# PEER layers with 392 dense prompt tokens instead of 400, eight more tokens gathered

## The chip, the cores and the metric

The kernel runs on one core of a Trainium2 chip. Its time is the device time of one launch in microseconds. Three runs of the kernel before gave 3549.24, 3555.11 and 3555.85 us; the median is 3555.11.

## The reference

The program is one inference step of a decoder trunk of two layers for 512 prompt tokens and 8 sample tokens, with a width of 1024, all in float32. Layer 0 mixes tokens with a gated MLP, layer 1 with sparse attention. Behind each of them stands a PEER layer, and the change is about that one:

```
q = (x @ w_q).reshape(T, 8 heads, 2, 128)
s1, s2 = q[:, :, 0] @ sub_k1.T, q[:, :, 1] @ sub_k2.T       # 128 keys each
v1, i1 = top_k(s1, 16);  v2, i2 = top_k(s2, 16)
top_s, top_pos = top_k(v1[..., :, None] + v2[..., None, :], 16)   # of 256 pairs
eidx = i1 * 128 + i2 at top_pos                             # 16 of 16384 experts a head
gate = softmax(top_s)
act  = gelu(einsum('thkd,td->thk', expert_u[eidx], x))
y    = einsum('thk,thkd->td', gate * act, expert_v[eidx])
```

## The kernel before

**Two ways to the same sum.** The prompt tokens 112 to 511 (`ND` = 400 of them, from `D0` = 112 on) take the dense way. All 16,384 experts are computed for them: in phase `s`, 128 slabs of 128 rows of `expert_u` are multiplied with the normed activations, the results go through GELU and to DRAM (`act_d`). The gates of these tokens, mostly zeros, are made as a table of 128 x 128 a token by a product of two one-hot matrices (`gates`, line 817), and go to DRAM as well (`gate_d`). In phase `y` activations and gates are read back in 16 groups of 8 slabs (`abuf`, `gbuf`), multiplied on VectorE (`weigh`), split into a high and a low part and multiplied with 128 slabs of `expert_v`. The prompt tokens 0 to 111 and the 8 sample tokens take the gathered way. They stand in 8 groups: group 0 holds the 8 samples (8 heads x 8 tokens = 64 partitions), groups 1 to 7 hold 16 prompt tokens each (8 x 16 = 128 partitions). For each of a group's 16 experts GpSimd gathers one row of `expert_u` per partition (an indirect DMA into one of four buffers `rows`), and VectorE takes its product with the token's activations (`dot`, line 1966): 128 dots a layer. In phase `y` the same is done with rows of `expert_v` (`value`, lines 1982 and 1985), and a matmul with `sel_t` or `sel_p` sums over the heads (`group_y`).

**Precision.** Every slab product is three float32r products, high by high, high by low and low by high. A dense slab is `dense` (line 681): 8 chunks x 3 = 24 matmuls of 128 x 128 by 400 columns into one bank. Slabs with all 520 tokens use `slab` (line 666): 48 matmuls of 260 columns. The weights come in through SP's queue into four buffers `raw`; ScalarE makes the high part (`w_hi`, line 1190), GpSimd (line 2411) or, in phase `y`, VectorE (line 2092) the low part `w_lo` in place. A slab's load is issued when the slab four before it is done.

**Order in phase s.** Each engine has its own program, and the order is written out by hand in slabs of TensorE. VectorE routes four blocks of 128 tokens (`routing`: top 16 of the scores, of the pair sums, the choice of experts, the gates). `between()` is called at twelve points of a routing, the hooks; each may hold a dot. Block b is routed in a window of `ROUTE_SLABS[b]` slabs; then TensorE turns the routes (`turn_route`, line 870) and 16 steps follow, each one slab and one half, that is eight tokens' gates: VectorE writes their one-hots (`one_hots`, lines 2001 and 2004), TensorE multiplies them (line 817), ScalarE takes them to `gout`, SP stores two halves at a time. `STEP_DOTS` says how many dots stand ahead of the one-hots of a step. Block 0 has no such steps: of its tokens only 112 to 127 are dense, and their two halves open block 1's steps. The halves left over follow block 3 (`LAST_STEPS`). `FETCH_AT` says at which slab GpSimd, after the slab's low part, issues each gather; the gather for dot i + 4 is due when dot i is. The activations of a group are turned to rows on TensorE by `group_h` (line 839) after all dots of the group before; the first dot of a group waits for it. After the third dot of a group VectorE spreads the next group's activations (`group_rows`, line 1952). The experts of groups 1 to 7 are ready after block 0 is routed: SP stores `route` to DRAM (`route_d`) and reads it back with partitions of head and token (`routeP`).

**Start of phase y.** VectorE weighs group 0 and takes its low parts before the phase. In the loop over the 128 slabs n = 8 j + c it weighs part c + 1 of group j + 1 (at c = 0 also part 0, which waits for the group's loads), makes the low part of slab n + 2, adds up the gathered values, and adds slab n to `x` (line 2121), which frees its bank.

**Attention tiles.** `attention()` multiplies 17 tiles of 128 columns with `slab` into two banks by turns. 15 of them are rotated: VectorE writes the scaled tile to `traw`, TensorE multiplies it with `rot` (line 973) into the tile's own bank, after the following slab, and VectorE multiplies the result with the sine (`rb`, line 2156), which frees the bank. The slab after the following one writes the same bank.

## Time and profile before

| | us |
|---|---|
| median of three runs | 3555.11 |
| the profiled execution | 3555.51 |
| its span | 3553.7 |
| TensorE matmuls busy | 3407.9 |
| VectorE busy | 2562.3 |
| GpSimd busy | 1879.6 |
| ScalarE busy | 1341.9 |

The profile shows one execution. Matmuls are pipelined, so the busy time of TensorE counts overlaps once and the mean of one matmul is longer than its share of the time. Times of single instructions are given from the span's start. Phase s of layer 0 lies at about 441 to 1134 us, phase y at 1134 to 1718, the attention tiles at 1718 to 1872; layer 1's PEER phases begin at about 2268 and 2962. The page's DMA line and the windows give how busy the 16 DMA engines were and what they moved.

### The profile page before, as it was taken

The page shows a single profiled execution, that of the slowest core. Times are in us where ns is not written, and L with a number is a line of the kernel's source. Part 1 is how long each engine was busy: PE and PEld are TensorE (multiplying, and loading weights), DVE is VectorE, ACT ScalarE, POOL GpSimd, SP SyncE. Part 2 cuts the span into 40 slices and gives each one's busy share as a digit, 9 for nine tenths or more (in the row PEclk, how much of TensorE's full clock was granted, in tenths as well). Part 3 has the DMA queues.
Part 4 walks back from the last instruction along what each step waited for, and adds up shares of the span by engine and source line. Part 5 has one row for each costly group of instructions (what it writes and reads, how often), then busy time and mean ns, then how long its engine had stood idle before and what let it go on. Part 6 is the DMA issues. An engine that isn't in the chain of part 4 may idle for free.

```text
span 3553.7 us, 60286 instructions
## 1 busy us (share of the span) xinstructions
PE 3407.9 (96%) x21261; PEld 3279.6 (92%) x21261; DVE 2562.3 (72%) x5458; ACT 1341.9 (38%) x1928; POOL 1879.6 (53%) x1236
## 2 busy tenths in 40 slices
PE   7999999999999999999888789999999999999998
PEld 7999999999999999999884459999999999999998
DVE  3342388898885788887568753598898867878885
ACT  3323243545453333333222363344444443333332
POOL 3434366565656655554452234466665666555552
PEclk9999999999999999999999899999999999999999
DMA  3222267888899999997335532468989899999994
GB/s 131 83 67 89 89 200 239 291 288 284 296 302 297 296 333 338 327 340 247 95 99 180 157 103 89 126 202 284 299 264 314 286 312 283 326 337 334 330 332 143
DMA packets 396185, 837.93 MB, mean 236 GB/s; under 512 B 58280, under 2 KB 218792, under 8 KB 395224
## 3 DMA queue, kind: packets, MB, share of 16 engines
q1 hardware_dynamic: 269232, 454.25, 39.2%
q0 software_dynamic: 73824, 264.29, 21.5%
q10 hardware_dynamic: 52880, 116.19, 9.7%
q8 instruction: 142, 2.33, 0.3%
q14 instruction: 107, 0.88, 0.1%
HBM read 724.80 MB, written 108.60 MB: 235 GB/s over the span
## 4 chain that ended last, share of the span: by engine, by line
PE 82%; DVE 8%; DMA 4%; issue 2%; ACT 2%; POOL 1%; ACTq 0%; SPq 0%; DVEq 0%; POOLq 0%
PE acc L681 54%; PE acc L666 16%; PE misc L817 5%; DMA raw<-slabs_in 2%; DMA rows<-u_in,expertP 1%; DVE rows L1966 1%; PE misc L922 1%; POOL w_lo L2411 1%; PE misc L1140 1%; PE misc L746 1%; DVE passed L2250 1%; PE misc L1104 0%; ACT w_hi L1190 0%; PE acc L1024 0%; DVE hot_gate L2004 0%
## 5 line engine op out<-in xcount | busy, mean ns | idle before, releaser
L2411 POOL TENSOR_TENSOR w_lo<-raw,w_hi 128x1024 fp32r<-128x1024 f32 x365 | 891.6, 2446 | 917.4 <-ACT w_hi L1190 916.1
L681 PE MATMUL acc<-h_hi,w_hi 128*128 128x400 f32 x3072 | 1071.6, 349 | 10.6 <-POOL w_lo L2411 6.2
L681 PE MATMUL acc<-h_hi,w_lo 128*128 128x400 f32 x3072 | 1060.5, 345 | 0.0
L681 PE MATMUL acc<-h_lo,w_hi 128*128 128x400 f32 x3072 | 1059.2, 345 | 0.0
L1190 ACT ACTIVATE w_hi<-raw 128x1024 fp32r<-128x1024 f32 x617 | 652.9, 1059 | 1074.6 <-DMA raw<-slabs_in 994.7
L681 PEld LDWEIGHTS acc<-h_hi,w_hi 128*128 128x128 f32 x3072 | 579.7, 189 | 15.4 <-ACT gelu L1322 7.7
L681 PEld LDWEIGHTS acc<-h_lo,w_hi 128*128 128x128 f32 x3072 | 580.1, 189 | 0.0
L681 PEld LDWEIGHTS acc<-h_hi,w_lo 128*128 128x128 f32 x3072 | 578.6, 188 | 0.1
L2092 DVE TENSOR_TENSOR w_lo<-raw,w_hi 128x1024 fp32r<-128x1024 f32 x252 | 360.2, 1429 | 176.7 <-ACT w_hi L1190 176.2
L1966 DVE CUSTOM_DVE_ANT_0 rows<-acc,rows 128x1024 f32<-128x1024 f32 (+1 forms) x256 | 309.8, 1220 | 172.1 <-DMA rows<-u_in,expertP 130.8
L681 PE MATMUL acc<-y_hi,w_hi 128*128 128x400 f32 x1024 | 357.1, 349 | 11.8 <-DVE x L2121 11.7
L681 PE MATMUL acc<-y_hi,w_lo 128*128 128x400 f32 x1024 | 355.7, 347 | 0.0
L681 PE MATMUL acc<-y_lo,w_hi 128*128 128x400 f32 x1024 | 355.4, 347 | 0.0
L1322 ACT ACTIVATE gelu<-acc 128x400 f32<-128x400 f32 x256 | 129.2, 505 | 581.4 <-PE acc L681 578.1
L2445 POOL DMA_INDIRECT rows<-v_in,expertP x224 | 219.2, 979 | 198.5 <-DVE acc L1985 107.7
L2453 POOL TENSOR_TENSOR h_lo<-abuf,h_hi 128x400 fp32r<-128x400 f32 x128 | 190.6, 1489 | 143.7 <-ACT h_hi L1369 142.6
L2004 DVE TENSOR_SCALAR hot_gate<-misc,idxT,gateT 128x128 f32<-128x128 f32 x800 | 263.4, 401 | 0.0
L2445 POOL DMA_INDIRECT rows<-u_in,expertP x224 | 218.4, 975 | 56.3 <-issue 26.6
L2453 POOL TENSOR_TENSOR y_lo<-abuf,y_hi 128x400 fp32r<-128x400 f32 x112 | 176.7, 1578 | 114.8 <-ACT y_hi L1369 113.6
L666 PE MATMUL acc<-h_hi,w_hi 128*128 128x260 f32 x912 | 191.8, 292 | 39.9 <-DVE rb L2156 16.7
L1343 ACT ACTIVATE gout<-misc 128x512 f32<-128x512 f32 x200 | 197.4, 1076 | 77.9 <-PE misc L817 77.9
L817 PE MATMUL misc<-hot_gate,hot 128*128 128x128 f32 x1600 | 202.4, 281 | 13.9 <-DVE hot_gate L2004 13.9
(353 smaller groups left out, 5522.4 us busy)
## 6 DMA issues: line engine op xcount, KB each, us to landing
raw<-slabs_in SPq DMA_DIRECT2D x617, 512.0 KB, 4.6
act_d<-gelu SPq DMA_DIRECT2D x256, 200.0 KB, 5.1
gate_d<-gout SPq DMA_DIRECT2D x50, 1024.0 KB, 7.0
abuf<-act_d ACTq DMA_DIRECT2D x128, 400.0 KB, 6.7
gbuf<-gate_d ACTq DMA_DIRECT2D x90, 384.0 KB, 6.4
gbuf<-gate_d ACTq DMA_DIRECT2D x30, 448.0 KB, 6.2
unit<-ck_in SPq DMA_DIRECT2D x72, 128.0 KB, 2.8
vquad<-cv_in SPq DMA_DIRECT2D x64, 128.0 KB
```

Source lines behind the costliest of these rows:

```text
L666: last = pe.matmul(acc[:, par, half, 0:HT], w[:, c, :], m(c)[:, half * HT:(half + 1) * HT], start=start and c == 0 and w is w_hi[r] and m ...
L681: last = pe.matmul(acc[:, 0, par, 0:ND], w[:, c, :], m(c), start=c == 0 and w is w_hi[r] and m is m_hi, stop=c == KC - 1 and w is w_lo[r])
L817: last = pe.matmul(misc[:, q, j * P:(j + 1) * P], hot1[par][:, t, :], hot_gate[par][:, t, :], start=True, stop=True)
L1190: act.activation(w_hi[r][:], raw[r][:], ACT.Copy).then_inc(hi_done, 1)
L1322: act.activation(gelu[:, par, :], acc[:, 0, par, 0:ND], ACT.Gelu_apprx_tanh).then_inc(acc_free_act, 1)
L1343: act.activation(gout[cpar][:, :, t0:t0 + 4].rearrange("p i t -> p t i"), misc[:, q, :].rearrange("p (t i) -> p t i", t=4), ACT.Copy).then ...
L1966: dve.tensor_tensor_reduce(out=row, in0=acc[0:n, 1], in1=row, scale=1.0, scalar=0.0, op0=ALU.mult, op1=ALU.add, accum_out=dots[0:n, g, k:k ...
L2004: last = dve.tensor_scalar(hot_gate[par][:, t, :], count_row, idxT[:, 1, t0 + t:t0 + t + 1], gateT[:, t0 + t:t0 + t + 1], ALU.is_equal, AL ...
L2092: dve.tensor_tensor(w_lo[r][:], raw[r][:], w_hi[r][:].bitcast(F32), ALU.subtract).then_inc(lo_done, 1)
L2411: pool.tensor_tensor(w_lo[r][:], raw[r][:], w_hi[r][:].bitcast(F32), ALU.subtract).then_inc(lo_done, 1)
L2445: pool.indirect_dma_start(out=rows[n % RB][0:rows_of], out_offset=None, in_=a[f"v{l}" if half else f"u{l}"], in_offset=bass.IndirectOffset ...
L2453: pool.tensor_tensor(y_lo[par][:, c, 0:ND], abuf[par][:, c, :], y_hi[par][:, c, 0:ND].bitcast(F32), ALU.subtract).then_inc(y_lo_done, 1)
```

## The change

392 prompt tokens take the dense way instead of 400. The eight tokens 112 to 119 join the samples in group 0, whose 128 partitions are now all used: the gathers, dots, values and turns of group 0 run on 128 partitions, and `sel_t` picks samples and prompt tokens apart. The number of groups, dots and gathers stays. Since the experts of these eight tokens are known only after block 0 is routed and its routes have been stored and read back (eight more loads, into `routeS`), no dot is left in window 0. All dots start in block 1's window, with new tables of hooks, steps, fetches and turns. Window 1 has 19 slabs instead of 20, and the scores of block 1 come two slabs earlier; group 1 is turned in block 1's first step, group 3 after ten slabs of window 2. In block 2 four dots follow the first one-hots. There are 49 halves a layer instead of 50. The gate table in DRAM and `gbuf` are flat, 24 whole pairs of halves and one single half at the end, and `weigh` is two multiplications, one of 384 columns and one of 8. In phase y the parts of group 1 are weighed from slab 1 on by `WEIGH_FIRST`. In the attention tiles the product with `rot` goes to banks 2 and 3 of `misc`; the next slab that writes the tile's bank no longer waits for `rb` of that tile, and each `rot` waits for the `rb` of the tile before.

```diff
-ND = 400
+ND = 392
+NMATE = D0 % TG
-        ROUTE_SLABS = [20, 20, 14, 14]
+        ROUTE_SLABS = [20, 19, 14, 14]
-        SLAB0 = [0, 20, 56, 86]
+        SLAB0 = [0, 20, 55, 85]
+        WEIGH_FIRST = [[], [0, 1], [2], [3], [4], [5], [6, 7], []]
-        WINDOW_DOTS = [16, 12, 16, 12]
+        WINDOW_DOTS = [0, 16, 16, 12]
+        HOOK_DOTS = [[0] * 12,
+                     [0, 0, 0, 0, 2, 2, 2, 2, 2, 2, 2, 2],
+                     [1, 2, 2, 2, 1, 0, 0, 1, 1, 1, 1, 0],
+                     [0, 1, 1, 1, 1, 1, 1, 1, 1, 1, 1, 2]]
-                     [0, 2, 2, 0, 1, 1, 2, 1, 1, 2, 1, 1, 2, 1, 1, 2],
-                     [0, 1, 2, 1, 1, 2, 1, 1, 2, 1, 1, 2, 1, 0, 2, 2],
-                     [0, 1, 2, 1, 2, 1, 2, 2, 1, 2, 2, 0, 1, 2, 1, 2]]
-        TURN_AFTER = {(1, 2): 2, (1, 15): 3, (2, 0): 4, (2, 12): 5, (3, 0): 6, (3, 10): 7}
-        WINDOW_AT = [[8, 10, 10, 11, 12, 13, 14, 15, 16, 18, 19, 19, 20, 20, 20, 21],
-                     [30, 31, 32, 33, 35, 36, 37, 38, 39, 39, 39, 40],
-                     [56, 57, 58, 60, 61, 62, 63, 64, 65, 67, 68, 68, 68, 69, 69, 70],
-                     [86, 87, 88, 90, 91, 92, 93, 93, 94, 96, 98, 99]]
+                     [0, 1, 2, 1, 2, 1, 2, 1, 2, 2, 2, 0, 2, 2, 2, 2],
+                     [0, 0, 2, 2, 2, 2, 0, 2, 2, 2, 1, 2, 2, 1, 2, 2],
+                     [0, 2, 2, 0, 2, 2, 2, 1, 2, 2, 1, 2, 2, 0, 2, 2]]
+        TURN_AFTER = {(1, 0): 1, (1, 10): 2, (2, 5): 4, (2, 15): 5, (3, 2): 6, (3, 12): 7}
+        TURN_IN = {2: (10, 3)}
+        WINDOW_AT = [[],
+                     [26, 26, 28, 28, 29, 29, 30, 31, 32, 32, 33, 34, 35, 35, 37, 37],
+                     [55, 58, 58, 59, 60, 61, 62, 63, 66, 67, 68, 69, 70, 70, 70, 71],
+                     [87, 88, 89, 90, 91, 91, 92, 92, 94, 95, 96, 97]]
-        FETCH_AT = [5] * RB + at_slab[:-RB]
-        FETCH_AT = [n if i < TOPK else max(n, 28) if i < NDOT else max(n, NK - 1) for i, n in enumerate(FETCH_AT)]
+        FETCH_AT = [24] * RB + at_slab[:-RB]
+        FETCH_AT = [n if i < NDOT else max(n, NK - 1) for i, n in enumerate(FETCH_AT)]
...
                     sp.dma_start(routeP[h * TG:(h + 1) * TG].rearrange("t g k s -> t g (k s)"),
+                    sp.dma_start(routeS[SR + h * NMATE:SR + (h + 1) * NMATE, :, 0], route_d[l][NSG * TG:D0, h]).then_inc(
+                        routeP_loaded, 16)
...
                 group_h(0)
-                s_only(17)
+                s_only(15)
                 scores(1, 0)
                 s_only(2)
                 scores(1, 1)
                 s_only(3)
                 turn_route(0)
-                s_only(4)
-                group_h(1)
...
+                    if s:
+                        pe.wait_ge(acc_free_dve, D0 + s + 2)
                     for half in range(2):
-                        last = pe.matmul(acc[:, par, half, 0:HT], rot[:], traw[par][:, half * HT:(half + 1) * HT],
+                        last = pe.matmul(misc[:, 2 + half, 0:HT], rot[:], traw[par][:, half * HT:(half + 1) * HT],
...
-                    slab(base + s, s % 4, s % 2, hh, hl, free=(acc_free_dve, D0 + s + 1),
+                    slab(base + s, s % 4, s % 2, hh, hl, free=(acc_free_dve, D0 + max(s, 2)),
...
+                            dve.scalar_tensor_tensor(expertS[SR:P], routeS[SR:P, 0, 0], float(NK), routeS[SR:P, 1, 0],
+                                                     ALU.mult, ALU.add).then_inc(expertP_done, 1)
-                        elif done[0] < last_dot and (b != 1 or hook[0] > 4):
+                        for _ in range(HOOK_DOTS[b][hook[0] - 1]):
                             next_dot()
...
                         one_hots(H0 + h, h * HG, h % 2, H0 + h < 2)
+                        while done[0] < last_dot:
+                            next_dot()
...
-                    dve.tensor_tensor(abuf[par][:, c, :].rearrange("p (n t) -> p n t", t=TG),
-                                      abuf[par][:, c, :].rearrange("p (n t) -> p n t", t=TG),
-                                      gbuf[par][:, :, c, :], ALU.mult).then_inc(y_mult, 1)
+                    dve.tensor_tensor(main, main, gbuf[par][:, 0:GT].rearrange("p (n g t) -> p n g t", g=GRP, t=TG)[:, :, c],
+                                      ALU.mult)
+                    dve.tensor_tensor(rest, rest, gbuf[par][:, GT:].rearrange("p (g t) -> p g t", g=GRP)[:, c],
+                                      ALU.mult).then_inc(y_mult, 1)
...
                     if j + 1 < J:
-                        if c == 0:
-                            weigh(j + 1, 0)
-                        if c + 1 < GRP:
-                            weigh(j + 1, c + 1)
+                        if j == 0:
+                            for k in WEIGH_FIRST[c]:
+                                weigh(1, k)
```

## Rows read from the trace of the kernel before

**Rows 1.** The page's costliest groups: busy us, mean ns of one, idle before.
```profile
L681 PE MATMUL acc<-h_hi,w_hi 128*128 128x400 f32 x3072 | 1071.6, 349 | 10.6 <-POOL w_lo L2411 6.2
```

**Rows 2.** The chain of waits in order of time: start us, length us, what.
```profile
349.13 86.52 PE acc L666 x720
...
569.20 34.95 PE acc L681 x192
...
1143.35 7.30 PE acc L681 x24
```

**Rows 3.** Who waited for whom, whole run, TensorE: us, times, longest us.
```profile
PE acc L666 <- DVE rb L2156: 16.7, 15, 4.0
...
PE acc L681 <- DVE x L2121: 14.9, 7, 4.6
PE misc L817 <- DVE hot_gate L2004: 13.9, 6, 2.7
```

**Rows 4.** Timeline of TensorE, layer 0, gate blocks: start us, us, instruction, idle before.
```profile
621.44 0.49 PE L870 MATMUL misc<-ident,route 128*128 128x128 f32 x3
...
629.05 1.16 PE L817 MATMUL misc<-hot_gate,hot 128*128 128x128 f32 x8 [2.72 <-DVE hot_gate L2004]
...
791.69 0.55 PE L870 MATMUL misc<-ident,route 128*128 128x128 f32 x3 [0.30 <-DVE route L1915]
...
798.23 1.06 PE L839 MATMUL acc<-ident,hS 128*128 128x128 f32 x8 [1.62 <-DVE dots L1966]
...
801.82 3.57 PE L817 MATMUL misc<-hot_gate,hot 128*128 128x128 f32 x15 [2.53 <-DVE hot_gate L2004]
...
810.92 1.95 PE L817 MATMUL misc<-hot_gate,hot 128*128 128x128 f32 x16
...
817.07 1.95 PE L817 MATMUL misc<-hot_gate,hot 128*128 128x128 f32 x16
```

**Rows 5.** Windows: length, busy us of PE, PEld, DVE, ACT, POOL, clock, DMA, GB/s.
```profile
797.00:908.00 111.00, 107.24 (x691) 106.97 (x692) 97.21 (x250) 55.56 (x69) 62.86 (x40) 0.97 0.87 281
...
1240.00:1340.00 100.00, 100.00 (x557) 100.00 (x556) 81.08 (x93) 33.63 (x45) 58.36 (x47) 1.00 0.92 334
```

**Rows 6.** DMA issues, whole run: count, median us from issue to landing.
```profile
rows<-u_in,expertP POOLq DMA_INDIRECT x224, 6.5
```

**Rows 7.** Timeline of VectorE, layer 0, routing and gate steps.
```profile
577.59 1.23 DVE L1966 CUSTOM_DVE_ANT_0 rows<-acc,rows 128x1024 f32<-128x1024 f32 x1 [11.06 <-DMA rows<-u_in,expertP]
...
721.16 3.18 DVE L1834 MAX8 keyv<-sc 128x8 f32<-128x128 f32 x16
728.58 1.23 DVE L1966 CUSTOM_DVE_ANT_0 rows<-acc,rows 128x1024 f32<-128x1024 f32 x1 [4.23 <-issue]
...
767.01 1.23 DVE L1966 CUSTOM_DVE_ANT_0 rows<-acc,rows 128x1024 f32<-128x1024 f32 x1
...
791.56 1.22 DVE L1966 CUSTOM_DVE_ANT_0 rows<-acc,rows 128x1024 f32<-128x1024 f32 x1
...
1070.17 1.22 DVE L2001 TENSOR_TENSOR hot<-misc,idxT 128x1024 f32<-128x1024 f32 x1
...
1073.85 1.22 DVE L2001 TENSOR_TENSOR hot<-misc,idxT 128x1024 f32<-128x1024 f32 x1
```

**Rows 8.** Timeline of TensorE, attention: a slab after a rotated tile.
```profile
1839.04 0.48 PE L666 MATMUL acc<-h_hi,w_hi 128*128 128x260 f32 x2 [0.88 <-DVE rb L2156]
```

**Rows 9.** DMA by queue, 1190 to 1250 us: packets, MB, share of 16 engines.
```profile
q0 software_dynamic: 1953, 7.09, 36.4%
```

**Rows 10.** Timeline of VectorE at the start of phase y, layer 0.
```profile
1132.39 0.16 DVE L2100 TENSOR_TENSOR weights<-dots,routeS 64x16 f32<-64x16 f32 x1
...
1137.95 0.57 DVE L2077 TENSOR_TENSOR abuf<-abuf,gbuf 128x400 f32<-128x400 f32 x1 [5.22 <-DMA abuf<-act_d]
```

**Rows 11.** DMA, 1130 to 1190 us: queue, packets, MB, share; issues, us to landing.
```profile
q0 software_dynamic: 1187, 3.90, 26.1%
...
rows<-v_in,expertS POOLq DMA_INDIRECT x15, 8.7
```

More of the change, by code:

```diff
@@ L477, in build @@
             for r, n in enumerate(STEP_DOTS[b]):
[L478 removed]
+                if (b, r) in TURN_AFTER:
                     assert len(at_slab) + n == TURN_AFTER[b, r] * TOPK
@@ L832, in group_h @@
                 def group_h(g):
-                    n = P if g else SR
+                    n = P
                     pe.wait_ge(hS_done, l * NGR + g + 1)
@@ L906, in peer @@
                             quarter_scores(b + 1, SCORE_STEPS.index(r))
-                    if b + 1 < NDB:
+                    if b + 1 in TURN_IN:
+                        slabs, g = TURN_IN[b + 1]
+                        s_only(slabs)
+                        group_h(g)
+                        s_only(ROUTE_SLABS[b + 1] - slabs)
+                    elif b + 1 < NDB:
                         s_only(ROUTE_SLABS[b + 1])
@@ L1443, in group_out @@
                 def group_out(g):
-                    n = P if g else SR
+                    n = P
                     act.wait_ge(rows_used, l * OPS + NDOT + (g + 1) * TOPK)
@@ L1973, in value @@
                 g, k = divmod(i, TOPK)
-                n = P if g else SR
+                n = P
                 u = l * OPS + NDOT + i
@@ L1990, in group_add @@
                 dve.wait_ge(s_y_done, l * NGR + g + 1)
-                t0, w = ((g - 1) * TG, TG) if g else (TP, TS)
-                dve.tensor_tensor(x[:, :, t0:t0 + w], x[:, :, t0:t0 + w],
-                                  misc[:, 2, 0:KC * w].rearrange("p (c t) -> p c t", c=KC), ALU.add).then_inc(
-                    s_y_added, 1)
+                y = misc[:, 2, 0:KC * TG].rearrange("p (c t) -> p c t", c=KC)
+                if g:
+                    parts = [(0, (g - 1) * TG, TG)]
+                else:
+                    parts = [(0, TP, TS), (TS, NSG * TG, NMATE)]
+                for c0, t0, w in parts:
+                    last = dve.tensor_tensor(x[:, :, t0:t0 + w], x[:, :, t0:t0 + w], y[:, :, c0:c0 + w], ALU.add)
+                last.then_inc(s_y_added, 1)
             def one_hots(half, t0, par, first):
@@ L2060, in peer @@
                         one_hots(H0 + h, h * HG, h % 2, H0 + h < 2)
+                        while done[0] < last_dot:
+                            next_dot()
                 for h in range(3 * HALF_STEPS, HALVES):
@@ L2107, in peer @@
                     if j + 1 < J:
-                        if c == 0:
-                            weigh(j + 1, 0)
-                        if c + 1 < GRP:
-                            weigh(j + 1, c + 1)
+                        if j == 0:
+                            for k in WEIGH_FIRST[c]:
+                                weigh(1, k)
+                        else:
+                            if c == 0:
+                                weigh(j + 1, 0)
+                            if c + 1 < GRP:
+                                weigh(j + 1, c + 1)
                     if n < NK - 2:
```

104 lines of the change are left out of this document (57 added, 47 removed).

## The prediction

> **What bounds the kernel now.** I read the page first. TensorE is busy 3407.9 of 3553.7 us, and its costliest groups are the dense matmuls of line 681: three of 3072 and three of 1024, 12,288 matmuls of 400 columns, of which one group stands in [rows 1]. The reader should not take 349 ns as their price, because they overlap. The chain of waits has stretches with nothing else in them: 192 matmuls of 400 columns in 34.95 us, a pitch of 182.0 ns, and 720 of 260 columns in 86.52 us, 120.2 ns [rows 2]. Next come TensorE's own waits [rows 3]: 16.7 us for `rb` in the attention tiles, 14.9 us for the adds into `x` in the value phase, 13.9 us for one-hots. Its timeline shows where those for one-hots fall: at the starts of the gate blocks [rows 4]. Last I read the engines beside it. The DMA engines are busy 0.87 of a gate block and 0.92 of the value phase [rows 5], and a gathered row set lands 6.5 us after its issue [rows 6]. VectorE's order in a routing window is in [rows 7]. So the end is set by TensorE nearly everywhere, with VectorE and DMA close behind; time goes where TensorE has less to do, and comes back where it must wait.
>
> **Columns.** From 260 to 400 columns the pitch grows by 61.8 ns, 0.442 ns a column; 8 columns fewer save 3.53 ns, and 12,288 matmuls 43.4 us [rows 1, 2]. At a granted clock of 1.00, the 2.4 GHz level, one column a cycle would save 3.33 ns, 41.0 us. I take **-42.2**, between both; a slab of 24 matmuls falls from 4.37 to 4.28 us. The Trainium skill (TensorE: Matmul & The Clock Gate, Back-to-back issue gap) gives sustained pitches of 81 ns at 128 columns and 131 ns at 512, 0.13 ns a column: by that the cut would be worth 12.8 us. The two pitches of this trace contradict it.
>
> **One half fewer.** A gate step lasts 6.15 us (810.92 to 817.07) [rows 4]; less 4.37 for its slab, the matmuls of the one-hots cost 1.78 us. Each layer has 49 halves for 50: **-3.6**.
>
> **Attention tiles.** `rot` no longer writes the bank that the next slab needs; that slab may start while VectorE still reads the product. Each tile shows a wait like the 0.88 us of [rows 8]; 15 of them make 16.7 us [rows 3]. What is late next is VectorE: it started `rb` of that tile 0.9 us before the slab at 1839.04 could start, has the sum and a reciprocal behind it, and is free again before the slab ends, so it hides; ScalarE's and GpSimd's parts are shorter still. The new wait of `rot` is for a read that ended a slab earlier. **-17** (bounds 0 and -20).
>
> **Dots moved.** Group 0 becomes 128 rows and its 16 dots leave window 0. There VectorE gets rid of 16 dots and a wait for rows, so block 0 is routed early; scores of block 1 come two slabs sooner. SP issues eight more small loads, in two lots of eight, past which it moves a slab load and a store of activations each; a slab load is issued four slabs ahead and lands in about one, so I give this nothing (if the cover fails, 2 us a layer).
>
> Block 1. The first gathers are due at slab 24 instead of 28, but routing begins earlier too; where VectorE waited 11.06 us for them [rows 7] I expect some 8. Routing by itself is 791.56 - 721.16 - 4.23 = 66.2 us with 12 dots and one spreading of rows [rows 7], so 51.4 without; with 16 dots, one spreading and the wait it is 51.4 + 18.2 + 1.1 + 8 = 79, against 20 slabs, 86 us, until TensorE asks for it. Before, four dots stood behind the routing and TensorE waited 2.72 us for the first one-hots [rows 4]; now none do. With the clock that such a wait costs, **-6** for both layers (bounds 0, -9).
>
> Block 2. Dot 48 opens group 3 and must wait until TensorE has turned its rows, which now happens after ten slabs of the window: 10 x 4.28 + 0.9 = 43.7 us after the window's first slab. From the dot at 767.01 to the end of routing at 791.56 VectorE took 24.6 us with five dots [rows 7]; now it has four and one group's rows to spread, the same. Routing ends at 68.3. TensorE arrives after 14 slabs and the turn, 60.9: it waits 7.4 us. Behind the waiting dot on VectorE stands `topd`, behind that on ScalarE the exponential and two high parts; these are 3 us late and the slab that needs them is 8 us off. Four dots now stand between the first and second one-hots: 4 x 1.14 + 3.68 (the pitch 1070.17 to 1073.85) = 8.2 against 6.06 for TensorE's step, some 1 us more. The old cost was 0.30 + 1.62 + 2.53 of waits [rows 4] and about 3 us of half clock (the gate matmuls took 3.57 for 1.95 us). New: 7.4 + 0.6 + 1 + 3 = 12.0 against 7.4, **+9** for both layers (bounds 0, if the clock stays up and VectorE's later dots hide behind the slower TensorE, and +16).
>
> Block 3 and the steps. The window is 60.0 us and routing 66.2, less the lead with which VectorE begins: in block 2 it was 791.69 - 61.2 - 721.16 = 9.3 us [rows 4, 7], and 6.2 are enough. 24, 28 and 24 dots sit in the steps where 20, 20 and 23 did; a two-dot step costs VectorE 3.68 + 2.28 = 5.96 of TensorE's 6.06. Gathers issued in block 2's steps rise from 21 to 29. At 1.46 us of all DMA engines each (36.4% of 60 us for 15) [rows 9] the load of that block, 0.87 x 111 = 97 us, becomes 109 in 107 us [rows 5]. I take **+3** (bounds -4, +16), as a few late rows like those of before.
>
> **Value phase, start.** VectorE stood 5.22 us in `weigh` of group 1 for its loads [rows 10]; behind it were the low parts of slab 2, and TensorE waited 4.6 us [rows 3] and then took 7.30 us for a slab worth 4.37 [rows 2]. Moved behind slab 0, that wait is uncovered from TensorE. Late next is the slab load itself, since the DMA engines are full here. And group 0's 16 gathers grow: 15 of 64 rows cost 26.1% of 60 us, 15 of 128 rows 36.4% [rows 9, 11], so 6.2 us of DMA time more in each layer. **-5** for both (bounds -16, +12).
>
> **Value phase, rest.** 256 more multiplications of 8 columns at about 0.1 us [rows 10] lie on VectorE, which is busy 0.81 [rows 5]: nothing. The DMA share goes from 0.92 to 0.94 as the slab shortens: **+4** for late loads (bounds 0, +21).
>
> Sum: -42.2 - 3.6 - 17 - 6 + 9 + 3 - 5 + 4 = -57.8. The profiled execution took 3555.51 us, 1.8 more than its span and 0.4 above the median of 3555.11: **3498**.
>
> **Rivals.**
> *The DMA engines hold the value phase at its old pace.* 334 GB/s at a share of 0.92 [rows 5] leave room up to 363, and the shorter slab wants about 341; that speaks against. For it: shares of 0.94 to 1.0 at the phase's start, with gathers that land after 8.7 us [rows 11]. The columns of this phase, 21.1 us, and the 5 at its start are lost: 3524. The Trainium skill (DMA: Bandwidth & Descriptors, Specifications) puts the HBM limit of a core at 358 GB/s; it would let 341 pass too.
> *Slower: rows late in two-dot steps.* 64 steps of the two layers have two dots. With four row buffers a buffer comes round every 12.1 us, and issue, dot, descriptor work and a `w_lo` ahead of it in GpSimd's queue need 11.3 at 6.5 us of landing. From about 7.5 us the gate matmuls wait in each. At the 8.7 us of [rows 11] it is 1.4 us; in 45 of the 64 steps 63 us, and some clock: 3565. Against: in 100 gate steps TensorE waited six times for one-hots, 13.9 us in all [rows 3].
> *The cuts are given back at block starts.* TensorE's waits in all blocks are as block 2's (-6 becomes +9, +3 becomes +10): 3520.
> *Columns are cheap*: TensorE's pitch has a floor that hides them, 0.13 ns each, 29.4 us less gained: 3527. These would be the Trainium skill's pitches, cited above. Against: at 260 columns the same pair of weight load and matmul passes in 120.2 ns [rows 2], so no such floor lies above that.
>
> **Numbers.** Forecast 68 in 100, DMA 15, late rows 7, block starts 7, cheap columns 3. Late rows can reach 3600, the forecast's good bounds 3465; I give 3472 to 3528. About 0.2% (7 us) is what a measurement can tell: faster 0.89, within 0.04, slower 0.07.
>
> **What would show it.** Right: a pitch near 178.5 ns; no wait for `rb` in the tiles; no wait at the first gates of block 1; one of 5 to 9 us for `route` at block 2; slabs 2 and 3 of the value phase without the 4.6 us. Wrong: a DMA share of 1.0 and slab loads over 9 us in the value phase, waits of gate matmuls in many steps, or a pitch above 180 ns.

## The result and the profile after

The changed kernel takes 3534.51 us, the median of five runs (3517.39 to 3535.91), beside 3555.11 for the kernel before (3549.24 to 3558.76): a ratio of 0.9931, 95% interval 0.9907 to 0.9955. In a second lot of runs it stood at 3528.29 against 3551.67, ratio 0.9927 (0.9905 to 0.9949). The medians lie 21 and 23 us apart, and the two intervals together reach from 16 to 34 us. The forecast was 3498, 57 us less than before, with a range from 3472 to 3528: the direction held, the size did not, and the time lies outside the range. Executions of one and the same kernel differ here by 10 us and more to either side, the longer ones mostly at a lower mean clock (0.975 to 0.979) than the shorter (0.983 to 0.987); so below, stretches of the traces are compared, and the medians only where they are far apart.

From here on the starts of the 512 dense slabs on TensorE's timeline cut both traces into stretches. They are worked out from the first and the last matmul of each, in us, layer 0 / layer 1:

| stretch | before | after | difference |
|---|---|---|---|
| start of s to first step of block 1 (40 and 39 slabs) | 180.8 / 180.8 | 172.5 / 172.5 | -8.3 / -8.3 |
| 16 steps of block 1 | 108.3 / 108.3 | 104.4 / 104.3 | -3.9 / -4.0 |
| window 2, with the wait for `route` | 62.0 / 61.6 | 70.3 / 69.5 | +8.3 / +7.9 |
| 16 steps of block 2 | 111.2 / 111.2 | 115.4 / 114.6 | +4.2 / +3.4 |
| window 3 | 66.5 / 66.0 | 64.4 / 63.9 | -2.1 / -2.1 |
| 16 steps of block 3 | 103.7 / 102.3 | 101.7 / 104.6 | -2.0 / +2.3 |
| rest of s (11 and 12 slabs) | 56.2 / 56.7 | 57.7 / 58.2 | +1.5 / +1.5 |
| **phase s** | 688.7 / 686.8 | 686.5 / 687.6 | -2.2 / +0.8 |
| phase y, 8 slabs | 44.5 / 42.6 | 39.5 / 39.3 | -5.0 / -3.3 |
| phase y, 120 slabs | 543.7 / 545.5 | 537.1 / 539.1 | -6.6 / -6.4 |
| layer 0's last slab to layer 1's first | 550.1 | 551.0 | +0.9 |

With 0.4 us more ahead of the first slab and 1.2 behind the last they give the spans, 3553.7 and 3533.5. So in this pair of traces all that was won was won in phase y, -21.3; both phases s together made 1.4, and the attention stage lost 0.9. The forecast had -18.7 for the two phases s, -22.1 for the two phases y and -17 for attention.

Who TensorE waited for, whole run, to be held against [rows 3]: us, times, longest us.

```profile
PE misc L831 <- DVE hot_gate L2034: 22.3, 16, 3.9
PE misc L884 <- DVE route L1937: 17.1, 4, 8.6
...
PE acc L695 <- DVE x L2162: 13.7, 17, 3.6
...
PE misc L985 <- issue: 7.2, 2, 5.0
```

The line for `rb` (16.7 us) is gone. In its place stand three that were smaller or not there: one-hots 22.3 for 13.9, `route` 17.1, nearly all of it at block 2, where it had been 0.3, and 7.2 in which the sums of a tile wait for ScalarE. The group of the costliest matmuls, the row of [rows 1], and two rows of the chain, start and length, the answer to [rows 2]:

```profile
L695 PE MATMUL acc<-h_hi,w_hi 128*128 128x392 f32 x3072 | 1065.0, 347 | 10.2 <-POOL w_lo L2452 5.8
```
```profile
349.51 86.50 PE acc L680 x720
...
540.74 72.98 PE acc L695 x408
```

72.98 us for 408 matmuls are 178.9 ns each for 182.0 before, and 86.50 / 720 = 120.1 ns at 260 columns is what it was. The eight columns are worth 3.1 ns by these rows and 3.4 by the mean over all unbroken pairs on the timeline (182.2 and 178.7 ns). The two sustained pitches that the Trainium skill gives (TensorE: Matmul & The Clock Gate, Back-to-back issue gap: 81 ns at 128 columns, 131 ns at 512) would have made it 1.0; the traces disagree.

Windows: length, busy us of PE, PEld, DVE, ACT, POOL, clock, DMA share, GB/s. Window 2 with the turn of its routes, the steps of block 2, and the value phase, as [rows 5]:

```profile
716.00:788.00 72.00, 63.43 (x365) 63.06 (x363) 63.39 (x265) 26.08 (x34) 47.37 (x28) 0.95 0.82 267
788.00:902.00 114.00, 106.01 (x674) 104.73 (x675) 94.17 (x207) 54.07 (x68) 64.89 (x44) 0.95 0.85 285
...
1240.00:1340.00 100.00, 100.00 (x566) 99.76 (x566) 82.68 (x118) 35.88 (x48) 59.15 (x48) 1.00 0.95 345
```

The value phase moves 345 GB/s for 334 at a DMA share of 0.95 for 0.92, and TensorE is busy throughout this window; the DMA engines let the shorter slab pass here. The steps of block 2 are another matter: TensorE lacks 8 of 114 us and its clock is 0.95.

### Block 2 on three timelines

TensorE, layer 0, start us, us, instruction, idle before; the rows that answer to [rows 4]:

```profile
787.99 0.90 PE L884 MATMUL misc<-ident,route 128*128 128x128 f32 x3 [8.57 <-DVE route L1937]
794.32 1.95 PE L831 MATMUL misc<-hot_gate,hot 128*128 128x128 f32 x16
802.97 2.05 PE L831 MATMUL misc<-hot_gate,hot 128*128 128x128 f32 x16 [2.44 <-DVE hot_gate L2034]
813.21 3.14 PE L831 MATMUL misc<-hot_gate,hot 128*128 128x128 f32 x13 [3.90 <-DVE hot_gate L2034]
```

VectorE, the same time. Only dots (L1992) and the first part of the one-hots (L2031) are copied:

```profile
762.37 1.22 DVE L1992 CUSTOM_DVE_ANT_0 rows<-acc,rows 128x1024 f32<-128x1024 f32 x1 [5.04 <-issue]
...
789.65 1.23 DVE L2031 TENSOR_TENSOR hot<-misc,idxT 128x1024 f32<-128x1024 f32 x1 [1.72 <-ACT gateT L1422]
...
793.34 1.22 DVE L1992 CUSTOM_DVE_ANT_0 rows<-acc,rows 128x1024 f32<-128x1024 f32 x1
...
794.48 1.22 DVE L1992 CUSTOM_DVE_ANT_0 rows<-acc,rows 128x1024 f32<-128x1024 f32 x1
...
798.00 1.23 DVE L1992 CUSTOM_DVE_ANT_0 rows<-acc,rows 128x1024 f32<-128x1024 f32 x1 [1.14 <-DMA rows<-u_in,expertP]
...
799.14 1.22 DVE L2031 TENSOR_TENSOR hot<-misc,idxT 128x1024 f32<-128x1024 f32 x1
...
806.85 1.22 DVE L1992 CUSTOM_DVE_ANT_0 rows<-acc,rows 128x1024 f32<-128x1024 f32 x1 [3.94 <-DMA rows<-u_in,expertP]
```

And GpSimd, whose queue holds low parts (L2452) and gathers (L2485):

```profile
790.64 2.38 POOL L2452 TENSOR_TENSOR w_lo<-raw,w_hi 128x1024 fp32r<-128x1024 f32 x1 [10.45 <-ACT w_hi L1209]
793.17 0.95 POOL L2485 DMA_INDIRECT rows<-u_in,expertP  x1
798.36 2.39 POOL L2452 TENSOR_TENSOR w_lo<-raw,w_hi 128x1024 fp32r<-128x1024 f32 x1 [4.24 <-ACT w_hi L1209]
800.91 0.95 POOL L2485 DMA_INDIRECT rows<-u_in,expertP  x1 [0.15 <-issue]
```

Read from the top: VectorE stands 5.04 us before dot 48, because TensorE turns that group's rows after ten slabs of the window (the row names no releaser; with the turn after twelve slabs, below, the same row stands 13.97). The routes come late by that and TensorE stands 8.57 us. A slab buffer comes free only when a slab is done, so through this wait no slab is loaded, and GpSimd stands 10.45 and then 4.24 us on low parts. Behind the first one-hots VectorE has four dots. Three find their rows in the buffers, the fourth waits 1.14 us. The buffers of the first three are free from 794.5 us on, but the gathers that refill them stand in GpSimd's queue behind the low part of 798.36 and leave at 800.91. The next dot gets its rows at 806.85, 5.9 us later, which is no more than the 6.5 us of [rows 6]: the rows left late, they did not travel long. The second and third one-hots are late, TensorE stands 2.44 and 3.90 us more, and its gate matmuls then run at 3.14 us for the 13 that the row holds, where sixteen take 1.95, the granted clock being at its lower level, 1.2 GHz.

### The profile page after: what moved, and what is told of

Read it like the earlier page. It is cut to its first block, busy times and chain, and to the rows that moved or that the text cites. A ratio compares the mean times of both kernels' runs of the same rounds, so it can differ in the third digit from the quotient of the medians.

```text
span 3533.5 us, 60285 instructions
## 1 busy us (share of the span) xinstructions
PE 3371.9 (95%) x21229; PEld 3230.7 (91%) x21229; DVE 2597.1 (74%) x5702; ACT 1323.7 (37%) x1914; POOL 1845.2 (52%) x1236
## 3 DMA queue, kind: packets, MB, share of 16 engines
q1 hardware_dynamic: 269930, 452.21, 38.9%
q0 software_dynamic: 77920, 281.07, 22.3%
## 4 chain that ended last, share of the span: by engine, by line
PE 72%; DVE 13%; DMA 6%; issue 3%; ACT 2%; POOL 2%; SPq 1%; ACTq 0%; DVEq 0%; POOLq 0%
PE acc L695 47%; PE acc L680 15%; PE misc L831 3%; DMA rows<-u_in,expertP 3%; DMA raw<-slabs_in 2%; DVE rows L1992 1%; DVE hot_gate L2034 1%; POOL w_lo L2452 1%; ACT w_hi L1209 1%; PE misc L1159 1%; DVE route L1925 1%; DVE misc L1921 1%; PE misc L939 1%; PE misc L1123 1%; DVE w_lo L2129 1%
## 5 line engine op out<-in xcount | busy, mean ns | idle before, releaser
L2452 POOL TENSOR_TENSOR w_lo<-raw,w_hi 128x1024 fp32r<-128x1024 f32 x365 | 896.0, 2458 | 926.8 <-ACT w_hi L1209 925.4
L695 PE MATMUL acc<-h_hi,w_hi 128*128 128x392 f32 x3072 | 1065.0, 347 | 10.2 <-POOL w_lo L2452 5.8
L695 PE MATMUL acc<-h_lo,w_hi 128*128 128x392 f32 x3072 | 1048.0, 341 | 0.0
L695 PE MATMUL acc<-h_hi,w_lo 128*128 128x392 f32 x3072 | 1044.6, 340 | 0.0
L1992 DVE CUSTOM_DVE_ANT_0 rows<-acc,rows 128x1024 f32<-128x1024 f32 x256 | 308.6, 1219 | 158.8 <-DMA rows<-u_in,expertP 125.9
L695 PE MATMUL acc<-y_hi,w_hi 128*128 128x392 f32 x1024 | 353.4, 345 | 11.5 <-DVE x L2162 10.2
L695 PE MATMUL acc<-y_lo,w_hi 128*128 128x392 f32 x1024 | 350.0, 342 | 0.0
L695 PE MATMUL acc<-y_hi,w_lo 128*128 128x392 f32 x1024 | 348.9, 341 | 0.0
L2485 POOL DMA_INDIRECT rows<-v_in,expertP x224 | 213.4, 953 | 252.6 <-DVE acc L2011 119.0
L1341 ACT ACTIVATE gelu<-acc 128x392 f32<-128x392 f32 x256 | 127.4, 497 | 545.1 <-PE acc L695 536.5
L2493 POOL TENSOR_TENSOR h_lo<-abuf,h_hi 128x392 fp32r<-128x392 f32 x128 | 179.5, 1402 | 134.5 <-ACT h_hi L1391 133.1
L2485 POOL DMA_INDIRECT rows<-u_in,expertP x224 | 214.3, 957 | 66.3 <-issue 31.9
L831 PE MATMUL misc<-hot_gate,hot 128*128 128x128 f32 x1568 | 198.7, 281 | 22.6 <-DVE hot_gate L2034 22.3
L831 PEld LDWEIGHTS misc<-hot_gate,hot 128*128 128x128 f32 x1568 | 191.9, 196 | 29.5 <-DVE hot_gate L2034 29.4
```

The source lines that it names most:

```text
L695: last = pe.matmul(acc[:, 0, par, 0:ND], w[:, c, :], m(c), start=c == 0 and w is w_hi[r] and m is m_hi, stop=c == KC - 1 and w is w_lo[r])
L831: last = pe.matmul(misc[:, q, j * P:(j + 1) * P], hot1[par][:, t, :], hot_gate[par][:, t, :], start=True, stop=True)
L1341: act.activation(gelu[:, par, :], acc[:, 0, par, 0:ND], ACT.Gelu_apprx_tanh).then_inc(acc_free_act, 1)
L1992: dve.tensor_tensor_reduce(out=row, in0=acc[0:n, 1], in1=row, scale=1.0, scalar=0.0, op0=ALU.mult, op1=ALU.add, accum_out=dots[0:n, g, k:k ...
L2452: pool.tensor_tensor(w_lo[r][:], raw[r][:], w_hi[r][:].bitcast(F32), ALU.subtract).then_inc(lo_done, 1)
L2485: pool.indirect_dma_start(out=rows[n % RB][:], out_offset=None, in_=a[f"v{l}" if half else f"u{l}"], in_offset=bass.IndirectOffsetOnAxis(a ...
```

## The experiments

All are edits of the changed kernel unless the heading says otherwise. Ratios are to the kernel before. Those of the first four runs share one lot of runs of it (median 3551.67), the next four another (3552.42), the last two a third (3554.44).

### The changed kernel again

> The changed kernel once more, unchanged, to see where its own executions differ: three of its five took 3534.5 to 3535.9 us at a mean clock of 0.978, two 3517.4 and 3519.5 at 0.981 and 0.983. Theory: the 17 us are TensorE's clock after the attention tiles, where the profiled execution shows 0.55, 0.87, 0.97 in three stretches of 50 us and the kernel before 0.69, 1.00, 1.00; an execution near 3518 us would show the sample attention (from the last tile to the next layer's first slab) 8 to 12 us shorter than 405.2 us. Rival: the difference is spread over the gate layers, whose late rows differ from one execution to the next; then the sample attention stays at 405 in either.

Measured: 3528.29 us (3522.01 to 3533.78). The profiled execution has a span of 3526.6 and 541.3 us between the layers' slabs, 9.7 less than the first trace of the same kernel; its phases s took 684.8 and 688.8, its phases y 581.1 and 577.5, together +3.1. Two stretches of the sample attention, first trace and then second:

```profile
1961.00:2011.00 50.00, 33.91 (x177) 20.57 (x175) 30.25 (x100) 16.43 (x53) 9.66 (x11) 0.55 0.25 82
2011.00:2061.00 50.00, 46.60 (x400) 23.00 (x398) 31.82 (x144) 31.06 (x112) 30.86 (x33) 0.87 0.56 171
```
```profile
1965.00:2015.00 50.00, 32.72 (x228) 20.76 (x226) 33.40 (x120) 20.90 (x71) 12.19 (x13) 0.69 0.31 94
2015.00:2065.00 50.00, 46.16 (x442) 24.02 (x434) 34.92 (x148) 34.71 (x115) 33.86 (x37) 1.00 0.64 192
```

The granted clock is 0.55 in the one and 0.69 in the other, then 0.87 and 1.00. So nearly 10 us of the first trace's attention stage are a difference between executions of one program and no effect of the change. Block 2 differs as well: its window took 70.3 us again in layer 0 but 73.7 in layer 1, where TensorE waited 12.0 us for `route`; the largest difference on VectorE's timeline is one instruction of the routing (L1910) that took 2.49 us in place of 0.28, and why is open. The theory holds for the trace; that it explains every spread of 17 us is not shown, since the other executions left no trace.

### `rot` alone, on the kernel before

```diff
+                    if s:
+                        pe.wait_ge(acc_free_dve, D0 + s + 2)
-                        last = pe.matmul(acc[:, par, half, 0:HT], rot[:], ...
+                        last = pe.matmul(misc[:, 2 + half, 0:HT], rot[:], ...
-                    slab(... free=(acc_free_dve, D0 + s + 1),
+                    slab(... free=(acc_free_dve, D0 + max(s, 2)),
-  dve.tensor_tensor(halves(rb[:]), acc[:, par, :, 0:HT], ...
+  dve.tensor_tensor(halves(rb[:]), misc[:, 2:4, 0:HT], ...
```

> The kernel before with one part of the change alone: rot writes the third and fourth misc bank and the next slab no longer waits for rb. The prediction gave it -17 us (0 to -20). Theory A (from the changed kernel's trace, where the tiles took 8.9 us less and 5.0 of a wait for sqh stood where 4.0 for rb had been): -9 us in the tiles, and what comes after depends on the clock, so -9 in all or 0 to -3 if the sample attention then runs at a lower clock as in the changed kernel. Rival B: the prediction's -17, and the missing 8 us are from other parts of the change.

Measured: 3543.14 us over twelve runs, ratio 0.9972 (0.9953 to 0.9991), 10 us less, between 3 and 17. Its attention stage took 538.4 us for 550.1. Who TensorE waited for between the layers:

```profile
PE misc L968 <- issue: 6.1, 3, 4.6
```

The 16.7 us for `rb` are gone and 6.1 for the sums of a tile have come. The theory read from the trace, -9, is the nearer; -17 lies at the very edge of the interval. The tiles by themselves, from the start of the first slab to that of the seventeenth, took 144.2 us in the kernel before, 129.7 with this edit, and 130.5 to 132.6 in seven traces of the changed kernel and its edits below that leave this part alone.

### Index keys behind the square

```diff
-                    if 1 <= s < 1 + 4 * NU:
-                        load_index_keys(s - 1)
                     if TILES[s][0] in NORMED:
                         ...
                     if s:
                         after(s - 1)
+                    if 1 <= s < 1 + 4 * NU:
+                        load_index_keys(s - 1)
```

> The changed kernel with ScalarE's loads of index keys (four issues of some 0.9 us in each tile) behind its square and root of the same tile instead of before them. In the changed kernel's trace one tile's square waited 3.4 us behind such issues, and TensorE 5.0 us for it, at the only place in the tiles where it stood long; the clock fell after it. Theory A: that wait shrinks to 1.6 us or less, -4 us, and with the clock that comes back -5 to -15. Theory B: the late slab (raw landed 12.4 us after ScalarE was free) is the cause and the order hides nothing: 0. Rival C: index keys arrive later and the sample attention's start waits for them: +2 to +5.

Measured: 3518.36 us (3507.01 to 3537.26), ratio 0.9890 (0.9867 to 0.9913). ScalarE around the square that TensorE waits for, in the changed kernel (ACTq rows are issues):

```profile
1767.96 1.06 ACT L1209 ACTIVATE w_hi<-raw 128x1024 fp32r<-128x1024 f32 x1 [12.43 <-DMA raw<-slabs_in]
1768.64 3.77 ACTq L1552 DMA_DIRECT2D ik<-cki_in  x4
1772.46 0.60 ACT L1566 ACTIVATE sqh<-acc 128x520 f32<-128x520 f32 x1 [3.44 <-issue]
```

and TensorE at that tile, first in the changed kernel and then with the edit:

```profile
1773.16 2.07 PE L985 MATMUL misc<-sqh,headones 128*128 128x260 f32 x4 [5.01 <-issue]
```
```profile
1773.73 1.11 PE L985 MATMUL misc<-sqh,headones 128*128 128x260 f32 x4 [1.24 <-issue]
```

The wait falls from 5.01 to 1.24 us, 3.8 of it being the issues. The 1.24 that stay are the late slab, so for this wait theory A holds with theory B as its rest. The tiles took 123.9 us by the measure above, and 123.4 and 123.2 in the two kernels further down that have this edit too: 7 to 9 us less than in the seven others. But the clock did not come back. From the seventeenth slab through the sample attention to the next slab of this kind, these three traces took 268.0, 264.4 and 266.5 us, where eight of the nine without the edit took 255.5 to 260.1, and the ninth, the first of the changed kernel, 269.7. Here are 70 us in the middle of that stretch, with the edit and then with the turn after 8 slabs (columns as in [rows 5]):

```profile
1955.50:2025.50 70.00, 54.55 (x308) 29.81 (x306) 40.99 (x155) 26.82 (x96) 21.80 (x23) 0.60 0.35 109
```
```profile
1952.70:2022.70 70.00, 51.13 (x408) 30.19 (x406) 49.58 (x192) 34.87 (x123) 26.94 (x29) 0.83 0.43 134
```

TensorE's waits there add up to 44 to 48 us in all of them, so rival C, late index keys, is out, and the difference is the granted clock, 0.60 for 0.83. In these traces, then, the gain was given back. Whether the edit brings the low clock with it or three executions fell that way is not shown; each of the three was the slowest execution of its kernel. The interval of the whole time touches the changed kernel's; the 10 us between the medians are likely and not shown.

### Turn after 8 slabs, and after 12

```diff
-        TURN_IN = {2: (10, 3)}
+        TURN_IN = {2: (8, 3)}        # the other kernel: (12, 3)
```

> The changed kernel with the rows of group 3 turned after 8 slabs of block 2's window instead of 10. VectorE stood 5.0 us before dot 48 for them, so route should be ready 4.5 to 5 us earlier and TensorE's wait of 8.6 and 7.7 us fall to about 3.5. Theory A, a wait of TensorE feeds on itself: while it stands, no slab buffer comes free, GpSimd's queue stands on a low part and the gathers behind it are issued late, so VectorE stands for rows and TensorE again for one-hots (2.4 and 3.9 us, with 0.86 of clock); with the first wait halved these go too, -20 us for both layers. Theory B, each wait is its own: -10 us, and the one-hot waits of steps 2 and 3 of block 2 stay. Theory C, the four dots between first and second one-hots are the whole cost: 0 to -4 us, since the later waits then come at the same place.

> The changed kernel with the rows of group 3 turned after 12 slabs of block 2's window instead of 10: dot 48 and what is behind it on VectorE come 8.6 us later in each layer. If each wait is its own (as the turn after 8 slabs showed: wait for route 4.8 and 3.1 us shorter, the 16 steps behind it unchanged at 115.5 and 115.2), the window grows from 70.3 and 69.5 to 79 us, and the steps stay at 115: +17 us. If a long wait feeds itself through GpSimd's queue, the steps grow as well, to 120 and more: +25.

| turn after | median | ratio | window 2 | steps of block 2 |
|---|---|---|---|---|
| 8 slabs | 3515.27 | 0.9899 (0.9872 to 0.9925) | 65.6 / 67.9 | 115.5 / 115.2 |
| 10 slabs | 3528.29 | 0.9927 (0.9905 to 0.9949) | 70.3 / 69.5, again 70.3 / 73.7 | 115.4 / 114.6, again 114.3 / 115.2 |
| 12 slabs | 3542.86 | 0.9980 (0.9962 to 0.9998) | 78.9 / 78.9 | 114.6 / 114.5 |

TensorE's waits in window and steps of layer 0, turn after 8 slabs:

```profile
PE misc L831 <- DVE hot_gate L2034: 7.5, 3, 5.3
PE misc L884 <- DVE route L1937: 3.8, 1, 3.8
```

Turn after 12 slabs:

```profile
PE misc L884 <- DVE route L1937: 9.7, 1, 9.7
PE misc L831 <- DVE hot_gate L2034: 7.1, 3, 4.2
PE acc L695 <- POOL w_lo L2452: 5.5, 1, 5.5
```

Theory A, that the first wait makes the later ones larger with its own length, falls: the steps behind it take 115 us whether TensorE waited 3.8, 8.6 or 9.7. Theory B holds, the window alone follows the turn, by 5 us in layer 0 and, in layer 1, by 2 to 6: there 1.3 us went to a new wait of TensorE for the dots ahead of a turn. At 12 slabs part of it shows as another wait of 5.5 us, for a low part that GpSimd began at 775.14 us, 1.6 us after dot 48 had ended. That dot frees the buffer of the gather ahead of it in the queue; this is read from the order of the queue, no row names it.

### The gathers one slab earlier; the four dots moved away

```diff
-                     [55, 58, 58, 59, 60, 61, 62, 63, 66, 67, 68, 69, 70, 70, 70, 71],
+                     [55, 58, 58, 59, 60, 61, 62, 63, 66, 67, 68, 69, 69, 69, 69, 70],
```

> The changed kernel with the gathers of dots 56 to 59 put one slab earlier into GpSimd's queue, ahead of a low part instead of behind it. In the changed kernel's trace that low part waits until 798.4 us for its slab while the buffers of these rows are free from 794.5; the gathers leave at 800.9 and VectorE stands 3.9 us for the first. Theory A, late gathers: VectorE's wait of 3.9 us goes, TensorE's waits for one-hots in steps 2 to 4 of block 2 (2.4 and 3.9 us) fall below 3, the 16 steps of block 2 take 110 to 112 us instead of 115.4, -8 to -10 us for both layers with the clock. Theory B, the four dots between the first and second one-hots: TensorE's 2.4 us stay, the 3.9 shrink to about 2: -4. Theory C, the block's own gathers keep the DMA engines full (0.98 to 1.03 here), so rows land as late as before: 0.

```diff
-        WINDOW_DOTS = [0, 16, 16, 12]
+        WINDOW_DOTS = [0, 16, 12, 12]
-                     [0, 0, 2, 2, 2, 2, 0, 2, 2, 2, 1, 2, 2, 1, 2, 2],
+                     [0, 1, 2, 2, 2, 2, 1, 2, 2, 2, 2, 2, 2, 2, 2, 2],
-        TURN_AFTER = {..., (2, 5): 4, ...}
+        TURN_AFTER = {..., (2, 7): 4, ...}
-                     [55, 58, 58, 59, 60, 61, 62, 63, 66, 67, 68, 69, 70, 70, 70, 71],
+                     [55, 58, 58, 59, 60, 61, 62, 63, 66, 67, 68, 69],
```

> The changed kernel with no dots between the first and second one-hots of block 2: its four go to steps 0 to 15, 28 dots there for 24, group 4 turned after step 7 instead of 5. Theory A, late gathers: the second one-hots come 4.6 us sooner, but rows are then due in the same places, so the waits move to later steps, 0 to -4 us for both layers. Theory B, the four dots: TensorE's wait of 2.4 us goes and the 3.9 falls to nothing, -10 us. Rival: with two dots in nearly every step VectorE has 5.96 of 6.06 us in each, catches up nothing, and the waits spread: +5.

Earlier gathers: 3517.60 us, ratio 0.9894 (0.9869 to 0.9918); the steps of block 2 took 110.1 and 111.0. Moved dots: 3511.72, ratio 0.9896 (0.9869 to 0.9923), 110.7 and 110.4. Window 2 took 70.3 or 70.4 us in both layers of both. With the earlier gathers GpSimd and then VectorE read, where the changed kernel had 798.36, 800.91 and 806.85:

```profile
795.66 0.93 POOL L2485 DMA_INDIRECT rows<-u_in,expertP  x1 [0.72 <-DVE dots L1992]
...
800.14 2.38 POOL L2452 TENSOR_TENSOR w_lo<-raw,w_hi 128x1024 fp32r<-128x1024 f32 x1 [1.06 <-ACT w_hi L1209]
```
```profile
804.12 1.23 DVE L1992 CUSTOM_DVE_ANT_0 rows<-acc,rows 128x1024 f32<-128x1024 f32 x1 [0.97 <-DMA rows<-u_in,expertP]
```

TensorE's steps with the dots moved:

```profile
786.85 0.90 PE L884 MATMUL misc<-ident,route 128*128 128x128 f32 x3 [8.57 <-DVE route L1937]
793.12 1.95 PE L831 MATMUL misc<-hot_gate,hot 128*128 128x128 f32 x16
799.19 1.95 PE L831 MATMUL misc<-hot_gate,hot 128*128 128x128 f32 x16
805.26 1.95 PE L831 MATMUL misc<-hot_gate,hot 128*128 128x128 f32 x16
```

The gather leaves 5.3 us sooner (795.66 for 800.91), VectorE's wait falls from 3.94 to 0.97, and the 16 steps lose 4 to 5 us. With the dots moved the first steps pass at 6.07 us without a wait. Each expectation was half met: the gathers gave 8.9 us over both layers, as the theory of late gathers said, but TensorE's one-hot waits fell to 4.0 and not below 3; the moved dots gave as much, 8.9, where that theory allowed 4. The spread is small beside that: in all twelve stretches with neither edit (the changed kernel twice, both turns, the keys behind the square and the weighing of the next section) the 16 steps took 114.3 to 116.1 us. Read together, the two are one cause seen from its two ends. Four dots in a row empty the four row buffers while the queue that refills them stands, and either an earlier refill or a later demand cures it.

### Group 1 weighed from slab 0

```diff
-        WEIGH_FIRST = [[], [0, 1], [2], [3], [4], [5], [6, 7], []]
+        WEIGH_FIRST = [[0, 1], [2], [3], [4], [5], [6], [7], []]
```

> The changed kernel with group 1 weighed from slab 0 on, as in the kernel before. By the prediction's own step VectorE stands some 5 us for the loads of that group with the low parts behind it, and TensorE waits 4.6 us after slab 2: the first eight slabs of a value phase take 43 instead of 39.4 us, +3.5 us in each layer, +7. Rival: the slab loads themselves are late there, with DMA shares near 1.0, and the order changes nothing: 0 to +2.

Measured: 3530.55 us, ratio 0.9937 (0.9914 to 0.9960), which can't be told from the changed kernel's. In its trace the first eight slabs of phase y took 42.1 and 41.8 us, beside 39.5, 39.3, 40.5 and 38.9 in the two traces of the changed kernel: +2.4 in each layer. That is less sure than it looks. The other edits keep the new order too, and over all 18 stretches with it the eight slabs took 38.5 to 42.3 us, 40.1 on average; so the order is worth about 2 us in each layer, some 4 in all, and the spread of the stretches is as large. The expectation failed on the cause: with the old order VectorE does not stand for the loads of group 1 at all, it weighs at once and then stands for gathered rows of `expert_v`:

```profile
1128.27 0.56 DVE L2113 TENSOR_TENSOR abuf<-abuf,gbuf 128x384 f32<-128x384 f32 x1
...
1134.44 1.29 DVE L2008 TENSOR_SCALAR misc<-rows,weights 128x1024 f32<-128x1024 f32 x1 [3.21 <-DMA rows<-v_in,expertS]
```

And in the changed kernel:

```profile
1134.53 1.29 DVE L2008 TENSOR_SCALAR misc<-rows,weights 128x1024 f32<-128x1024 f32 x1 [1.10 <-DMA rows<-v_in,expertS]
1138.30 1.29 DVE L2011 SCALAR_TENSOR_TENSOR misc<-rows,weights,misc 128x1024 f32<-128x1024 f32 x1 [2.48 <-DMA rows<-v_in,expertS]
1139.49 0.56 DVE L2162 TENSOR_TENSOR x<-x,acc 128x392 f32<-128x392 f32 x1
```

TensorE waits 3.56 us for that add, where it waited 4.6 before and 5.0 with the old order. In either order it is the first gathered rows of `expert_v` that hold it, and no longer the loads of group 1. Which part of the change made those loads come in time is open.

### The edits together

One kernel has the turn after 8 slabs, the earlier gathers and the keys behind the square; in the other the moved dots take the place of the earlier gathers.

> The changed kernel with three edits together: group 3 turned after 8 slabs, the gathers of dots 56 to 59 one slab earlier, ScalarE's loads of index keys behind its square. Sum of the parts if each wait is its own: -10 for the turn (its trace showed the wait for route 3.8 and 4.6 us instead of 8.6 and 7.7), -8 for the gathers, -5 to -10 for the order in the tiles: 3528 - 25 = 3503. If one late row follows the other whatever is moved, 3515, where the two single edits stand already.

> Three edits on the changed kernel: group 3 turned after 8 slabs, the four dots behind the first one-hots of block 2 moved into its steps, ScalarE's loads of index keys behind its square. The version with the earlier gathers in place of the moved dots stood at 3500.4 us, its steps of block 2 at 114.4 and 109.2 us; moved dots took them to 110.7 and 110.4. If the moved dots are the steadier cure: 3496 to 3500. If both only shift the same late rows: 3500 to 3505.

Measured: 3500.40 us (3491.81 to 3511.12), ratio 0.9845 (0.9820 to 0.9870), and 3500.67 (3500.43 to 3508.79), ratio 0.9855 (0.9829 to 0.9882). Both beat the changed kernel by 28 us, clear of its interval, and the kernel before by 52 and 54. The medians nearly add up: -13, -11 and -10 by the single edits, -28 together. The traces of these executions, each the slowest of its five, account for less: beside the two traces of the changed kernel the two phases s together lost some 18 us in the first and 13 in the second, and the attention stage took 536.6 and 538.7 us, where three kernels without the keys' edit (the two turns and the old weighing) had 536.6 to 537.4. The window took 62.7 and 67.4 us in the first, 66.1 and 65.2 in the second; the steps of block 2 took 114.4 and 109.2, and 110.0 and 108.6. In layer 0 of the first a late row came back. Its gather left at 787.26 us, behind a low part that had waited until 784.73, and after the shorter wait the dots were there sooner than it could land:

```profile
792.83 1.23 DVE L1992 CUSTOM_DVE_ANT_0 rows<-acc,rows 128x1024 f32<-128x1024 f32 x1 [3.16 <-DMA rows<-u_in,expertP]
```

The moved dots look like the steadier cure, 108.6 to 110.7 us in all four stretches with them, though no difference of the medians says so.

## Why the prediction was wrong

**Columns, -42.2: right.** 182.2 to 178.7 ns over 12,288 matmuls is some 42 us, and 38 by the chain's rows. The rival of cheap columns is out.

**One half fewer, -3.6: right.** The rest of phase s has one slab more and one half fewer: +4.28 for the slab, -0.9 for the columns of eleven, leaves -1.8 of the measured +1.5 in each layer.

**Attention tiles, -17: mis-sized, -10 by the medians, -12 to -14 in the tiles of the traces.** The wait for `rb` went, as said. "What is late next is VectorE [...] ScalarE's and GpSimd's parts are shorter still" failed. ScalarE's own work is short, but its queue also issues four loads of index keys a tile, 3.5 to 3.8 us, ahead of the square. One tile's wait of 4.0 us had been put down to `rb` and came back as 5.0 under another name. The experiment on the kernel before gave -10 us. That the profiled pair shows +0.9 is the clock behind the tiles, 0.55 in the first trace against 0.69 in the second, whose stage took 541.3 us.

**Block 1, -6: right.** No wait for first one-hots (1.2 and 0.8 us for later ones); its steps lost 3.9 us, 1.4 of it columns, so -5 for both layers.

**Block 2, +9: the step that failed, +29.** Window 2 grew by 8.3 and 7.9 us, 9.5 and 9.1 with the columns it should have saved; the steps grew by 4.2 and 3.4, 5.6 and 4.8 with theirs. The wait for `route` was forecast at 7.4 us and is 8.6 and 7.7 (12.0 once in the second trace), so that term was nearly right. What was wrong was the balance behind it: "New: 7.4 + 0.6 + 1 + 3 = 12.0 against 7.4" (where the 0.6 comes from it does not say). By it the steps should have got shorter, 1 + 3 us of waits and lost clock for the old 1.62 + 2.53 + 3. The four dots between the first and second one-hots were priced by VectorE's pitch alone, 8.2 against 6.06 us, "some 1 us more". Rows were taken as landed. They were not: the sum had no term for GpSimd's queue, where the gathers stand behind a low part that waits for a slab that waits for TensorE. TensorE's waits for one-hots in the steps came to 8.0 us in layer 0 and 7.1 in layer 1, with the clock at 0.95. By the experiments the window's share is eased by the turn (-4.7 us in layer 0, -1.6 in layer 1) and the steps' share by rows in time (-4 to -5 in each layer), and one does not touch the other.

**Block 3, steps, +3: right,** about +1: windows -0.9 each after the columns, steps -0.6 and +3.7.

**Value phase, start, -5: right in size, not in cause.** The first eight slabs lost 8.3 us over both layers in the profiled pair, 1.3 of it columns; over all traces with the new order and the four stretches of the two kernels without the change to this phase they lost 6, columns included, and the order by itself gave some 4, within the spread. Next in line was not the slab load but the rows of group 0, and in the changed kernel they come last in the old order too.

**Value phase, rest, +4: too small,** +6.8 in the profiled pair and nearer +9 over all traces, inside its bounds of 0 and +21: 120 slabs lost 6.6 and 6.4 us in the pair, 5.6 on average over all traces, where the columns should give 9.9. Where these microseconds go was not looked into.

**The rivals.** DMA does not hold the value phase at its old pace: the phases y lost 21 us in the first trace and 18 in the second. Rows late in two-dot steps, slower: the mechanism exists, but at the block's start and not in every step. The given-back cuts at block starts is the rival that came nearest, 3520, and it had 7 chances in 100: it is right on block 2 and wrong on blocks 1 and 3. With block 2 at +29, the tiles at -10 and the rest of the value phase at +9 the sum is -57.8 + 20 + 7 + 5 = -26, beside medians of -21 and -23, and the second trace of the changed kernel is 27.1 us shorter than the trace before. The profiled pair's -20.2 would be -31 with the attention stage at -10 instead of its +0.9; that takes the better phase y of the two traces and is too much.

## What to carry to other kernels

When work is moved to just behind a wait, ask what else stood still through that wait: here the queue that refills the row buffers did, so a burst of four dots cost the time of its refill and not only its pitch. Price a burst by how many filled buffers it finds and by what stands ahead of the refill in its queue. When a wait is put down to one releaser, look for the second that ended just before it; and count an engine's DMA issues as its work, since four issues of some 0.9 us ahead of a 0.6 us square were what the next engine waited for.

## What was not expected of the hardware

The sample attention runs at a granted clock that differs between executions of one program: 0.55 or 0.69 over the same 50 us, 0.87 or 1.00 over the next. It makes nearly 10 us of 3530 between two traces of one program, as much as a real edit here. Over the twelve traces of all kernels the stretch behind the tiles took 255.5 to 260.1 us in eight and 264.4 to 269.7 in four, with TensorE's waits the same 44 to 48 us: in the eight the longest run at the lower clock, in the middle, was 24 to 31 us, in the four 48 to 58.

How long TensorE waited did not by itself say what its clock did. After a wait of 8.6 us the transposes behind it took 0.90 us, and 0.55 after one of 1.13 us (in the first of the two joined kernels), but also 0.55 after one of 4.55 us (in the second). Sixteen gate matmuls, 1.95 us without a wait, took 3.4 to 3.8 after waits of 3.9 to 5.7 us, the 1.2 GHz level for most of them or all; after 2.44 us they took 2.05 in the changed kernel, while after 2.53 us in the kernel before fifteen took 3.57 [rows 4].
